# An order of work in the memory stage: the samples' softmax later, their score products in halves

## The chip, the cores and the metric

The kernel runs on one core of a Trainium2 chip. The metric is device microseconds of that core for one launch. Engines: TensorE (PE), VectorE (DVE), ScalarE (ACT), GpSimd (POOL) and SyncE (SP, which here only starts transfers). Each takes its own instructions in order and waits on semaphores for the others.

## The reference

One decoder layer for two groups of requests with shared weights: a prompt of 512 tokens and 8 samples of one token each, width 1024, all in float32. It has a token mixer, cross-attention into 256 memory tokens, and a SwiGLU feed-forward. The change is in the cross-attention:

```
mem_kv:      m = rmsnorm(mem);  mk = m @ w_mk;  mv = m @ w_mv        # 256 tokens, 4 heads of 256; prompt only
mem_attend:  q = h @ w_xq
             s = einsum('bthd,bmhd->bhtm', q, mk) / 16               # scores, per head
             p = softmax(s);  o = einsum('bhtm,bmhd->bthd', p, mv);  return o @ w_xo
```

The prompt's keys and values are computed from `mem_prompt` and are outputs as well. The 8 samples have keys and values of their own in a cache (`cache_mem_k`, `cache_mem_v`), 1 MB per sample and kind.

## The kernel before

**Products.** A float32 product is made of three matmuls on rounded parts, high times high, high times low and low times high. Whatever enters a product is split first: ScalarE writes the high part, VectorE the low one (source minus high). Weights come in slots of 128 x 1024 floats (512 KB): SyncE loads one into one of 2 raw buffers, ScalarE makes its high part in two halves, VectorE its low part, in one of 3 homes. The load of slot s waits until the low part of slot s-2 is made, since they share the raw buffer; the high part of slot s waits until TensorE has used slot s-3. The memory stage has 16 slots in the order of `MEM_TILES`: `mm 0` to `mm 3`, two halves of `mv 0`, `mm 4`, `mm 5`, two halves of `mv 1`, `mm 6`, `mm 7`, and so on. `key_tile(j)` and `split_next(key)` split the slot two places behind the one that they name: `key_tile(2)` on ScalarE and VectorE splits the first half of `mv 0`, `split_next(("mv", 0, 0))` splits `mm 4`.

**The stage.** Eight query tiles (`xq`, 8 slots) come first. Then, on TensorE: `key_tile(j)` makes 128 columns of keys (24 matmuls), two tiles to a head; `mem_scores(h)` the prompt's scores of a head (24 matmuls) into two banks; `key_rows(h)` turns the keys for the output; `value_tile(h)` makes the values from two slots; `turned(h)` transposes the probabilities; `mixed(h)` multiplies them with the values. Around it VectorE takes the maxima (`cmaxes(h)`), ScalarE the exponentials (`cexps(h)`, with the first load of the exponential's table ahead of them), and VectorE scales them (`normalised(h)`). Both have functions of the same names (`key_tile`, `value_tile`, `turned`, `mixed`) for their part of each tile: copy out and high part on ScalarE, low part on VectorE.

**The samples.** Their scores are not made by TensorE. ScalarE writes a head's queries of the 8 samples to memory (`query_rows`), POOL broadcasts them to all partitions (`broadcast_rows`, into 4 buffers `q_by`), and VectorE multiplies with the cached keys and sums (line 2327), two products for a pair of head and sample. `SPREADS` puts the 32 pairs in 9 groups of two parts each; `scores_of(g)` makes group g, three or four pairs, and `spent(engine, g, i)` waits until part i of it is made, when the broadcast buffer and at times a cached key's slot are free. Then the softmax over the samples' scores, which lie over the partitions: `cmx` (a maximum on VectorE), `cmxt` (a transpose on TensorE), the top and `cdiag` (VectorE), `cmxb` (a broadcast by TensorE), `cdif` (a difference on VectorE), an exponential (ScalarE), `csum` (VectorE), `ctot` (a sum over partitions on TensorE), `cpnorm` (VectorE). After it `cached_values(b)` multiplies with the cached values, one sample each.

**What sets the order.** The order is written out by hand, once for each engine (TensorE in lines 3416 to 3500, VectorE 2339 to 2445, ScalarE 1648 to 1690, SyncE 1025 to 1046), and the lists `bank_order`, `val_order` and `split_order` give each result the number that waits count by. There are 7 banks in turn: a result's bank must be free of the one seven places earlier. SyncE's loads of cached keys and values (`load_kv`) stand between those of weights, some behind a wait for products that are made (`spent`), because the values take over slots of keys.

Of the kernel before, what the change touches and what calls it, by code (L numbers as in the profile page):

```python
# [18 lines left out]
ACT = mybir.ActivationFunctionType  # L19
# [4 lines left out]
KD = D // P  # L24
TP = 512
NB = 8
# [143 lines left out]
def bank_order():  # L170

    o = [("gain",), ("xs",)] + [("xt", c) for c in range(5)]
    o += [("in", 0, f) for f in (0, 1)] + [("xt", 6), ("xt", 7), ("bc",)] + [("in", 1, f) for f in (0, 1)]
    o += [("passed", f) for f in (0, 1)]
    for m in range(2, 10):
        o += [("in", m, f) for f in (0, 1)]
        if m == 2:
            o += [("gain2",), ("cp",)] + [("wuk", h) for h in range(NH)]
        if m == 3:
            o += [("rotk", f) for f in (0, 1)]  # L180
        if m == 4:
            o += [("ssq", "nkv")]
        if m == 6:
            o += [("bk",)]
        if m == 8:
            o += [("ct", t) for t in range(4)]
        if m == 9:
            o += [("kt",), ("smp",)]
    o += [("us",), ("ut",)]
    o += [("kn", h) for h in range(NH)]  # L190
    o += [("py", g, f) for g in (3, 2, 1, 0) for f in (0, 1)]
    o += [("ssq", "nq")]
    o += [("ur", p, f) for p in (0, 1) for f in (0, 1)]
    for h in range(NH):
        if h < 2:
            o += [("rotq", h, f) for f in (0, 1)]
        o += [("un", h, f) for f in (0, 1)]
    us = units()
    o += [("s",) + us[0], ("v", 0), ("s",) + us[1], ("qls",), ("v", 1), ("s",) + us[2], ("v", 2), ("qd",), ("s",) + us[3],
          ("v", 3), ("snew",)]  # L200
    for n in range(len(us)):
        o += [("pt",) + us[n]]
        if n + 4 < len(us):
            o += [("s",) + us[n + 4]]
        if n == len(us) - 3:
            o += [("o", 0, 0)]
    o += [("own",)]
    for b in range(NB):
        o += [("sc", b)]
        if b < 3:  # L210
            o += [("o", b + 1, 0)]
    o += [("o", 4, 0), ("o", 5, 0), ("ot",), ("uvs",)]
    for n, m in enumerate(OUT_ORDER):
        o += [("o", m, f) for f in (0, 1) if f or m >= NFIRST]
        if n == MT_AT:
            o += [("mt", k) for k in range(4)]
    def mem_scores(h):
        return [("cs", h, 0), ("cs", h, 1)]

    def mixed(h):  # L220
        return [("cpv", h, 0), ("cpv", h, 1)]

    def turned(h):
        return [("cpt", h, 0), ("cpt", h, 1)]

    for m in range(KD):
        o += [("xq", m, f) for f in (0, 1)]
        if m == 0:
            o += [("ssq", "nxs")]
        if m in (2, 4, 6):  # L230
            o += [("qt", m // 2 - 1)]
        if m == 6:
            o += [("ssq", "nx")]
    o += [("mm", 0), ("qt", 3)] + [("mm", j) for j in (1, 2, 3)]
    o += mem_scores(0) + [("mn", 0)] + [("mv", 0), ("mm", 4), ("cmxt",), ("mm", 5), ("cmxb",)]
    o += mem_scores(1) + [("mn", 1)] + turned(0) + [("mv", 1), ("ctot",)] + mixed(0) + [("mm", 6), ("mm", 7)]
    o += mem_scores(2) + [("mn", 2)] + turned(1) + mem_scores(3) + [("mn", 3), ("mv", 2)] + mixed(1)
    o += turned(2) + [("mv", 3)] + mixed(2) + turned(3) + [("xo", 0, 0), ("cot",)] + mixed(3)
    o += [("xo", m, f) for m in range(KD) for f in (0, 1) if m or f]
    for j in range(J0 - 1):  # L240
        o += [("g", j, 0), ("g", j, 1)]
        if j == 0:
            o += [("ssq", "nf")]
        o += [("u", j, 0)]
        if j == 0:
            o += [("bf",)]
        o += [("u", j, 1)]
    o += [(key, J0 - 1, f) for f in (0, 1) for key in ("g", "u")]
    for j in range(J0, NF):
        o += [("sx", j), ("sy", j), ("sz", j)]  # L250
    for j in range(NF, U_LAST):
        o += [("sx", j), ("sy", j), ("sz", j)] if is_block(j) else [("d", j, m, f) for m in tiles_of(j) for f in (0, 1)]
    o += [("y", 0, 0), ("y", 1, 0), ("e", KD - 2), ("e", KD - 1)] + [("y", t, 0) for t in (2, 3, 4)] + [("y", 0, 1), ("y", 3, 1)]
    o += [("z", 0), ("z", 2), ("z", 4)]
    return o

def val_order():
# [24 lines left out]
    for n, m in enumerate(OUT_ORDER):  # L283
# [2 lines left out]
            o += [("ms", "mem")]  # L286
        if n == MT_AT - 2:
            o += [("memn",)]
    o += [("ms", "nxs"), ("rx",), ("ms", "nx"), ("rxp",), ("cnegm", 0), ("cmx",), ("cdiag",), ("cpn", 0), ("cdif",), ("csum",)]
    o += [("cnegm", 1), ("cpn", 1), ("cpnorm",), ("cnegm", 2), ("cnegm", 3), ("cpn", 2), ("cpn", 3)]  # L290
    for m in range(KD):
        if m == 3:
            o += [("T13", J0)]
# [106 lines left out]
def build(nc, a, consts, outs):  # L400
# [4 lines left out]
    with ctx:  # L405
# [568 lines left out]
        def _(sp):  # L974
# [55 lines left out]
            for i in range(2, len(MEM_TILES) + 2):  # L1030
# [4 lines left out]
                if i == 8:  # L1035
                    spent(sp, 7, 1)
                    load_kv(NB)
                elif i in (9, 10, 11):
                    spent(sp, 8, 1)
                    load_kv(NB + i - 8)  # L1040
                elif i in (12, 13):
                    full(sp, ("cs", 1, 1))
                    load_kv(NB + i - 8)
                elif i in (14, 15):
                    sp.wait_ge(v_used, i - 13)
                    load_kv(NB + i - 8)
# [198 lines left out]
        def _(act):  # L1245
# [16 lines left out]
            def after(key):  # L1262
                act.wait_ge(val, VAL[key] + 1)
# [383 lines left out]

            key_tile(0)
            query_rows(3)
            for j in (1, 2, 3):  # L1650
                key_tile(j)
            split_next(("mv", 0, 0))
            split_next(("mv", 0, 1))
            cexps(0)
            key_rows(0)
            value_tile(0)
            key_tile(4)
            key_tile(5)
            after(("cdif",))
            act.activation(Pcs[:, :, :, :], Dc[:, :, :, :], ACT.Exp, scale=MEM_SCALE).then_inc(c_exp, 1)  # L1660
            cexps(1)
            key_rows(1)
            turned(0)
            value_tile(1)
            mixed(0)
            key_tile(6)
            key_tile(7)
# [257 lines left out]
        def _(dve):  # L1925
# [390 lines left out]
                            gain(G_MEM + 2 * k + 1))  # L2316

            def scores_of(g):

                for i, members in enumerate(SPREADS[g]):
                    slot_ = (2 * g + i) % QBUF
                    dve.wait_ge(q_in[slot_], 16 * ((2 * g + i) // QBUF + 1))
                    for n, (h, b) in enumerate(members):
# [13 lines left out]
            for m in range(KD):  # L2338
# [13 lines left out]
                if m == 6:  # L2352
# [3 lines left out]
                    step(dve.reciprocal(rx[:, 0:4], rx[:, 0:4]))  # L2356
                    dve.tensor_scalar(x_scale[:, 0], rx[:, 0:4], MEM_SCALE, None, ALU.mult).then_inc(rx_made, 1)
                    value(("rxp",), dve.tensor_scalar(x_scale[:, 1], rx[:, 0:4], -MEM_SCALE, None, ALU.mult))
                if m >= 3:
                    scores_of(m - 3)  # L2360

# [34 lines left out]
                for dc in (0, 1):  # L2397
                    low(("cpv", h, dc), A_lo[:, 2 * h + dc, 0:TP], full(dve, ("cpv", h, dc)), A_hi[:, 2 * h + dc, 0:TP])

            for j in range(4):  # L2400
                key_tile(j)
                if j == 3:
                    split_next(("mv", 0, 0))
                scores_of(5 + j)
            cmaxes(0)
            value(("cmx",), dve.tensor_reduce(cols[:, 3], Sc[:, :, :, :].rearrange("p b j h -> p b h j"), AX, ALU.max))
            split_next(("mv", 0, 1))
            b = full(dve, ("cmxt",))
            top = cols[0:NB * NH, 2].rearrange("p b h -> p (b h)")[:, 0:1]
            frees(dve.reduce_max(top, b[0:NB * NH, 0:P], AX), ("cmxt",))  # L2410
            freed(dve, ("cmxt",))
            value(("cdiag",), dve.tensor_scalar(diag[0:NB * NH, :], ident[0:NB * NH, 0:NB * NH], top, None, ALU.mult))
            value_tile(0)
            normalised(0)
            key_tile(4)
            key_tile(5)
            b = full(dve, ("cmxb",))
            frees(dve.tensor_copy(cols[:, 3].rearrange("p b h -> p (b h)"), b[:, 0:NB * NH]), ("cmxb",))
            freed(dve, ("cmxb",))
            value(("cdif",), dve.tensor_tensor(Dc[:, :, :, :], Sc[:, :, :, :], inner(cols[:, 3], 2), ALU.subtract))  # L2420
            dve.wait_ge(c_exp, 1)
            value(("csum",), dve.tensor_reduce(cols[:, 6], Pcs[:, :, :, :].rearrange("p b j h -> p b h j"), AX, ALU.add))
            cmaxes(1)
            turned(0)
            value_tile(1)
            normalised(1)
            mixed(0)
            ins = dve.reciprocal(cols[:, 7].rearrange("p b h -> p (b h)"), full(dve, ("ctot",))[:, 0:NB * NH])
            frees(ins, ("ctot",))
# [428 lines left out]
        def _(pe):  # L2858
# [557 lines left out]
            split(("mt", 3))  # L3416
            key_tile(0)
            query_rows(3)
            for j in (1, 2, 3):
                key_tile(j)  # L3420
            mem_scores(0)
            key_rows(0)
            value_tile(0)
            key_tile(4)
            b = out(("cmxt",))
            after(("cmx",))
            filled(pe.transpose(b[0:NB * NH, 0:P], cols[:, 3].rearrange("p b h -> p (b h)"), ident[:, :]), ("cmxt",))
            key_tile(5)
            b = out(("cmxb",))
            after(("cdiag",))  # L3430
            filled(pe.matmul(b[:, 0:NB * NH], ones[0:NB * NH, :], diag[0:NB * NH, :], start=True, stop=True), ("cmxb",))
            mem_scores(1)
            key_rows(1)
            turned(0)
            value_tile(1)
            b = out(("ctot",))
            after(("csum",))
            filled(pe.matmul(b[:, 0:NB * NH], ones[:, :], cols[:, 6].rearrange("p b h -> p (b h)"), start=True, stop=True), ("ctot",))
            mixed(0)
            key_tile(6)  # L3440
            key_tile(7)
            cached_values(0)
# [297 lines left out]
```

## Time and profile before

| | us |
|---|---|
| median of 3 runs (lowest, highest) | 796.64 (796.23, 796.9) |
| profiled execution | 799.21 |
| its span | 797.4 |
| TensorE busy | 761.1 (95%) |
| VectorE busy | 593.8 (74%) |
| ScalarE busy | 394.2 (49%) |
| POOL busy | 125.9 (16%) |
| mean DMA rate | 138 GB/s |

The profile is of one execution; its times are microseconds from the start of the span. The memory stage lies between 294 and 390 us. A row of a timeline has the start, the time taken, the engine, the line, what is written and read, and in brackets the idle time ahead of it and what ended that.
### The profile page before, as it was taken

To read this page: it belongs to the slowest core of one execution; us is meant where nothing else is said; L and a number is where in the kernel's file an instruction comes from. 1 tells how busy PE (TensorE), PEld (TensorE's weight loads), DVE (VectorE), ACT (ScalarE), POOL (GpSimd) and SP (SyncE) were. 2 spreads that over 40 slices of the span, in tenths; PEclk is the share of its full clock that TensorE was granted. 3 is DMA by queue.
4 is the path that set the end of the run, shared out by engine and by line. 5 is a ranking of instruction groups with operands and counts; after the bars stand their busy time and mean duration, and the time that the engine had idled before them with its cause. 6 is when DMAs were issued, how large, how long until landed. Compare 5 with 4: busy or idle time off the path is not lost. (4 is left out here: it accounts for less than half of the span.)

```text
span 797.4 us, 16199 instructions
## 1 busy us (share of the span) xinstructions
PE 761.1 (95%) x6264; PEld 728.3 (91%) x6264; DVE 593.8 (74%) x1170; ACT 394.2 (49%) x850; POOL 125.9 (16%) x179
## 2 busy tenths in 40 slices
PE   5999998898999998899999999999999999999996
PEld 5999897875899997898899999999999999999996
DVE  5778674677466798666489799888888869876664
ACT  5523776422264433665344356555555558433344
POOL 0376303331004821000046000000000000000000
PEclk9999999999999999899999999999999999999998
DMA  9423333453596668894243214433333333333303
GB/s 266 117 54 86 103 107 143 149 182 136 156 317 221 201 188 242 275 366 164 79 122 107 73 43 116 115 101 108 104 102 106 103 93 107 110 106 117 114 10 108
DMA packets 141521, 109.95 MB, mean 138 GB/s; under 512 B 9477, under 2 KB 133470, under 8 KB 138365
## 3 DMA queue, kind: packets, MB, share of 16 engines
q1 hardware_dynamic: 134574, 90.65, 37.4%
q0 software_dynamic: 3104, 14.68, 5.5%
q10 hardware_dynamic: 3767, 3.59, 1.3%
q8 instruction: 50, 0.82, 0.4%
q14 instruction: 26, 0.21, 0.1%
HBM read 103.93 MB, written 5.20 MB: 137 GB/s over the span
## 5 line engine op out<-in xcount | busy, mean ns | idle before, releaser
L1951 DVE TENSOR_TENSOR wlo<-wraw,whi 128x512 fp32r<-128x512 f32 (+1 forms) x178 | 129.4, 763 | 45.6 <-ACT whi L1254 35.8
L2889 PE MATMUL ps<-B_hi,whi 128*128 128x260 f32 x384 | 110.0, 286 | 3.3 <-DVE xT L1996 1.6
L2891 PE MATMUL ps<-B_hi,wlo 128*128 128x260 f32 x384 | 108.5, 282 | 0.0
L2890 PE MATMUL ps<-B_lo,whi 128*128 128x260 f32 x384 | 108.4, 282 | 0.0
L1254 ACT ACTIVATE whi<-wraw 128x512 fp32r<-128x512 f32 (+1 forms) x138 | 77.8, 615 | 54.6 <-DMA wraw<-in_w_xq_dram 11.4
L2889 PE MATMUL ps<-A_hi,whi 128*128 128x260 f32 x264 | 76.4, 290 | 0.5 <-ACT kn_lo L1348 0.3
L2889 PEld LDWEIGHTS ps<-B_hi,whi 128*128 128x128 f32 x384 | 72.3, 188 | 4.4 <-DVE xT L1996 1.8
L2890 PE MATMUL ps<-A_lo,whi 128*128 128x260 f32 x264 | 75.2, 285 | 0.0
L2891 PE MATMUL ps<-A_hi,wlo 128*128 128x260 f32 x264 | 75.1, 284 | 0.0
L2891 PEld LDWEIGHTS ps<-B_hi,wlo 128*128 128x128 f32 x384 | 72.4, 189 | 0.0
L2890 PEld LDWEIGHTS ps<-B_lo,whi 128*128 128x128 f32 x384 | 72.3, 188 | 0.0
L3526 PE MATMUL ps<-B_lo,whi 128*128 128x260 f32 x236 | 66.6, 282 | 0.0
L3526 PE MATMUL ps<-B_hi,whi 128*128 128x260 f32 x236 | 66.6, 282 | 0.0
L3526 PE MATMUL ps<-B_hi,wlo 128*128 128x260 f32 x236 | 66.6, 282 | 0.0
L1695 ACT ACTIVATE whi<-t 128x512 fp32r<-128x512 f32 x66 | 41.0, 628 | 39.3 <-PE ps L3526 20.6
L2889 PEld LDWEIGHTS ps<-A_hi,whi 128*128 128x128 f32 x264 | 50.5, 191 | 3.0 <-issue 1.7
L1951 DVE TENSOR_TENSOR wlo<-t,whi 128x512 fp32r<-128x512 f32 x66 | 45.3, 687 | 9.4 <-ACT whi L1695 9.4
L2890 PEld LDWEIGHTS ps<-A_lo,whi 128*128 128x128 f32 x264 | 50.4, 191 | 0.1
L2891 PEld LDWEIGHTS ps<-A_hi,wlo 128*128 128x128 f32 x264 | 50.4, 191 | 0.0
L2890 PE MATMUL ps<-h_lo,whi 128*128 128x260 f32 (+1 forms) x164 | 46.3, 283 | 0.0
L3526 PE MATMUL ps<-S_hi,whi 128*128 128x260 f32 x160 | 45.3, 283 | 1.1 <-ACT upv L1760 1.1
L3526 PE MATMUL ps<-S_lo,whi 128*128 128x260 f32 x160 | 45.1, 282 | 0.0
(560 smaller groups left out, 2395.5 us busy)
## 6 DMA issues: line engine op xcount, KB each, us to landing
kv_slot<-in_cache_mem_k_dram SPq DMA_DIRECT2D x8, 1024.0 KB, 8.7
kv_slot<-in_cache_mem_v_dram SPq DMA_DIRECT2D x8, 1024.0 KB, 7.6
wraw<-in_w_out_dram SPq DMA_DIRECT2D x14, 512.0 KB, 4.2
wraw<-in_w_up_dram SPq DMA_DIRECT2D x12, 512.0 KB, 4.5
xraw<-in_w_gate_dram SPq DMA_DIRECT2D x20, 256.0 KB, 3.9
xraw<-in_w_up_dram SPq DMA_DIRECT2D x10, 512.0 KB, 4.1
wraw<-in_w_in_dram SPq DMA_DIRECT2D x9, 512.0 KB, 4.1
wraw<-in_w_gate_dram SPq DMA_DIRECT2D x18, 256.0 KB, 4.4
```

The costliest lines, as they stand in the source:

```text
L1254: act.activation(whi[:, home(s), c0:c1], wraw[:, s % RAW, c0:c1], ACT.Copy).then_inc(w_hi, 1)
L1695: act.activation(piece_at(name, j)[0], piece_source(name, j), ACT.Copy).then_inc(piece_hi, 1)
L1951: return dve.tensor_tensor(dst, src, high.bitcast(F32), ALU.subtract)
L2889: pe.matmul(dst, left[0], right[0], start=first, stop=False)
L2890: pe.matmul(dst, left[0], right[1], start=False, stop=False)
L2891: return pe.matmul(dst, left[1], right[0], start=False, stop=last)
L3526: ins = pe.matmul(b[:, 0:TH], x[:, c], y[:, k, :], start=first and k == n == 0, stop=k == 3 and n == 2, skip_group_check=True)
```

## The change

The order of the same instructions is changed on four engines. The lists of orders at the top change with them; they are left out below.

```diff
 # SyncE
                 if i == 8:
                     spent(sp, 7, 1)
                     load_kv(NB)
-                elif i in (9, 10, 11):
+                elif i in (10, 11):
                     spent(sp, 8, 1)
-                    load_kv(NB + i - 8)
+                    load_kv(NB + 2 * i - 19)
+                    if i == 10:
+                        load_kv(NB + 2)
 # ScalarE
             key_tile(0)
             query_rows(3)
-            for j in (1, 2, 3):
-                key_tile(j)
+            key_tile(1)
+            key_tile(2)
+            cexps(0)
+            key_rows(0)
+            key_tile(3)
             split_next(("mv", 0, 0))
             split_next(("mv", 0, 1))
-            cexps(0)
-            key_rows(0)
             value_tile(0)
             key_tile(4)
             key_tile(5)
-            after(("cdif",))
-            act.activation(Pcs[:, :, :, :], Dc[:, :, :, :], ACT.Exp, scale=MEM_SCALE).then_inc(c_exp, 1)
             cexps(1)
             key_rows(1)
             turned(0)
             value_tile(1)
+            after(("cdif",))
+            act.activation(Pcs[:, :, :, :], Dc[:, :, :, :], ACT.Exp, scale=MEM_SCALE).then_inc(c_exp, 1)
             mixed(0)
 # VectorE
-            def scores_of(g):
-                for i, members in enumerate(SPREADS[g]):
+            def scores_of(g, *parts):
+                for i in parts or (0, 1):
+                    members = SPREADS[g][i]
...
-                if m >= 3:
+                if 3 <= m < KD - 1:
                     scores_of(m - 3)
...
-            for j in range(4):
-                key_tile(j)
-                if j == 3:
-                    split_next(("mv", 0, 0))
-                scores_of(5 + j)
+            key_tile(0)
+            scores_of(4)
+            key_tile(1)
+            scores_of(5, 0)
             cmaxes(0)
+            key_tile(2)
+            scores_of(5, 1)
+            key_tile(3)
+            scores_of(6)
+            split_next(("mv", 0, 0))
+            normalised(0)
+            scores_of(7, 0)
+            split_next(("mv", 0, 1))
+            scores_of(7, 1)
+            value_tile(0)
+            key_tile(4)
+            scores_of(8, 0)
+            key_tile(5)
+            scores_of(8, 1)
             value(("cmx",), dve.tensor_reduce(cols[:, 3], Sc[:, :, :, :].rearrange("p b j h -> p b h j"), AX, ALU.max))
-            split_next(("mv", 0, 1))
+            cmaxes(1)
+            turned(0)
             b = full(dve, ("cmxt",))
...
-            value_tile(0)
-            normalised(0)
-            key_tile(4)
-            key_tile(5)
+            value_tile(1)
             b = full(dve, ("cmxb",))
...
+            normalised(1)
             dve.wait_ge(c_exp, 1)
             value(("csum",), ...)
-            cmaxes(1)
-            turned(0)
-            value_tile(1)
-            normalised(1)
             mixed(0)
 # TensorE
             key_tile(0)
             query_rows(3)
-            for j in (1, 2, 3):
-                key_tile(j)
+            key_tile(1)
+            key_tile(2)
             mem_scores(0)
             key_rows(0)
+            key_tile(3)
             value_tile(0)
             key_tile(4)
+            key_tile(5)
+            mem_scores(1)
+            key_rows(1)
+            turned(0)
...
-            key_tile(5)
+            value_tile(1)
...
-            mem_scores(1)
-            key_rows(1)
-            turned(0)
-            value_tile(1)
+            mixed(0)
...
-            mixed(0)
             key_tile(6)
             key_tile(7)
             cached_values(0)
```

## Rows read from the trace of the kernel before

**Rows 1.** Stretches: their length, then each engine's busy time (instructions), PEclk, DMA share, GB/s.
```profile
296.00:324.40 28.40, 22.52 (x186) 21.68 (x185) 24.95 (x92) 10.50 (x22) 3.44 (x6) 1.00 0.79 246
...
324.80:331.60 6.80, 6.05 (x27) 5.76 (x27) 4.03 (x9) 6.24 (x17) 0.00 (x0) 0.50 0.75 221
...
344.50:392.00 47.50, 47.50 (x424) 40.27 (x423) 26.84 (x47) 25.04 (x56) 0.00 (x0) 1.00 0.54 193
```

**Rows 2.** The timeline of TensorE in the memory stage.
```profile
305.48 0.39 PE L2889 MATMUL ps<-mT_hi,whi 128*128 128x256 f32 x1 [2.18 <-DVE wlo L1951]
...
315.82 0.38 PE L3367 MATMUL ps<-whi,mT_hi 128*128 128x256 f32 x1 [1.20 <-DVE wlo L1951]
...
318.96 0.38 PE L2889 MATMUL ps<-mT_hi,whi 128*128 128x256 f32 x1
...
324.44 0.27 PE L3427 MATMUL ps<-ident,cols 128*32 128x128 f32 x1 [2.39 <-DVE cols L2406]
...
325.55 0.58 PE L2889 MATMUL ps<-mT_hi,whi 128*128 128x256 f32 x1 [0.84 <-DVE wlo L1951]
...
335.77 0.36 PE L3367 MATMUL ps<-whi,mT_hi 128*128 128x256 f32 x1
...
341.64 0.48 PE L2889 MATMUL ps<-PTc_hi,mv_hi 128*128 128x512 f32 x1
...
344.50 0.28 PE L2889 MATMUL ps<-mT_hi,whi 128*128 128x256 f32 x1
```

**Rows 3.** The timeline of VectorE.
```profile
298.86 1.29 DVE L1951 TENSOR_TENSOR wlo<-wraw,whi 128x512 fp32r<-128x512 f32 x2
...
314.46 1.29 DVE L1951 TENSOR_TENSOR wlo<-wraw,whi 128x512 fp32r<-128x512 f32 x2
...
319.28 0.42 DVE L2327 CUSTOM_DVE_ANT_0 prod<-kv_slot,q_by 128x256 f32<-128x256 f32 x1
...
319.75 0.43 DVE L2327 CUSTOM_DVE_ANT_0 prod<-kv_slot,q_by 128x256 f32<-128x256 f32 x1
...
334.59 1.41 DVE L2382 TENSOR_REDUCE cstat<-ps 128x2 f32<-128x512 f32 x2
...
340.22 1.29 DVE L1951 TENSOR_TENSOR PTc_lo<-ps,PTc_hi 128x512 fp32r<-128x512 f32 x2 [4.03 <-ACT PTc_hi L1260]
...
344.23 0.69 DVE L1951 TENSOR_TENSOR mv_lo<-ps,mv_hi 128x512 fp32r<-128x512 f32 x1 [0.26 <-ACT mv_hi L1260]
```

**Rows 4.** The timeline of ScalarE.
```profile
308.45 1.15 ACT L1254 ACTIVATE whi<-wraw 128x512 fp32r<-128x512 f32 x2 [5.42 <-DMA wraw<-in_w_mv_dram]
...
319.95 0.63 ACT L1254 ACTIVATE whi<-wraw 128x512 fp32r<-128x512 f32 x1 [1.86 <-DMA wraw<-in_w_mk_dram]
...
321.13 1.28 ACT L1626 ACT_TABLE_LOAD   x1
...
324.20 0.56 ACT L1626 ACTIVATE Pc<-ps,cstat,x_scale 128x256 f32<-128x256 f32 x1 [1.79 <-DVE cstat L2383]
...
327.46 0.60 ACT L1609 ACTIVATE kv_nat<-ps 128x512 f32<-128x512 f32 x1 [0.48 <-ACT kv_nat L1266]
...
330.37 1.13 ACT L1254 ACTIVATE whi<-wraw 128x512 fp32r<-128x512 f32 x2
...
342.01 1.15 ACT L1254 ACTIVATE whi<-wraw 128x512 fp32r<-128x512 f32 x2 [0.37 <-DMA wraw<-in_w_mk_dram]
```

**Rows 5.** The timeline of SyncE, which issues the loads.
```profile
300.18 0.37 SPq L982 DMA_DIRECT2D wraw<-in_w_mv_dram  x1
...
319.34 0.51 SPq L1015 DMA_DIRECT2D kv_slot<-in_cache_mem_v_dram  x1
...
325.52 0.37 SPq L982 DMA_DIRECT2D wraw<-in_w_mv_dram  x1
...
333.45 0.37 SPq L982 DMA_DIRECT2D wraw<-in_w_mk_dram  x1
```

**Rows 6.** DMA issues of the page: form, count, KB each, median us to landing.
```profile
kv_slot<-in_cache_mem_v_dram SPq DMA_DIRECT2D x8, 1024.0 KB, 7.6
```

More of the change, by code:

```diff
@@ L233, in bank_order @@
             o += [("ssq", "nx")]
-    o += [("mm", 0), ("qt", 3)] + [("mm", j) for j in (1, 2, 3)]
-    o += mem_scores(0) + [("mn", 0)] + [("mv", 0), ("mm", 4), ("cmxt",), ("mm", 5), ("cmxb",)]
-    o += mem_scores(1) + [("mn", 1)] + turned(0) + [("mv", 1), ("ctot",)] + mixed(0) + [("mm", 6), ("mm", 7)]
+    o += [("mm", 0), ("qt", 3), ("mm", 1), ("mm", 2)]
+    o += mem_scores(0) + [("mn", 0), ("mm", 3), ("mv", 0), ("mm", 4), ("mm", 5)]
+    o += mem_scores(1) + [("mn", 1)] + turned(0) + [("cmxt",), ("mv", 1), ("cmxb",)] + mixed(0) + [("ctot",), ("mm", 6), ("mm", 7)]
     o += mem_scores(2) + [("mn", 2)] + turned(1) + mem_scores(3) + [("mn", 3), ("mv", 2)] + mixed(1)
@@ L288, in val_order @@
             o += [("memn",)]
-    o += [("ms", "nxs"), ("rx",), ("ms", "nx"), ("rxp",), ("cnegm", 0), ("cmx",), ("cdiag",), ("cpn", 0), ("cdif",), ("csum",)]
-    o += [("cnegm", 1), ("cpn", 1), ("cpnorm",), ("cnegm", 2), ("cnegm", 3), ("cpn", 2), ("cpn", 3)]
+    o += [("ms", "nxs"), ("rx",), ("ms", "nx"), ("rxp",), ("cnegm", 0), ("cpn", 0), ("cmx",), ("cnegm", 1), ("cdiag",), ("cdif",)]
+    o += [("cpn", 1), ("csum",), ("cpnorm",), ("cnegm", 2), ("cnegm", 3), ("cpn", 2), ("cpn", 3)]
     for m in range(KD):
```

## The prediction, written before the result was known

> **What bounds it now.** I read the stretches first, then each engine in order of time, with what ended its waits. From 344.5 to 392 us TensorE is busy for every microsecond. Before that it is not: 22.5 of 28.4 us from 296 to 324.4 us, and from 324.8 to 331.6 us it runs at the lower of its two clock levels, 1.2 GHz (a granted clock of 0.50), 27 matmuls in 6.05 us of busy time against 186 in 22.5 us [rows 1]. Its waits are 2.18 us ahead of `key_tile(3)`, 1.20 us inside `value_tile(0)`, both for low parts of weights from VectorE, 2.39 us at `cmxt` for `cmx`, and 0.84 us ahead of `key_tile(5)` for a low part again [rows 2]; together 6.6 us, and the change is about these. VectorE is late with them: a score product starts every 0.47 us (319.28, 319.75), so a (head, sample) pair costs 0.93 us and a group of four pairs 3.7 us, and such a group stands ahead of the next low part, as ahead of that at 314.46 [rows 3].
>
> But another chain ends last. `cmaxes(1)` starts at 334.59, its exponentials follow on ScalarE, and the low parts of the turned probabilities, started at 340.22, end at 341.51; `mixed(0)` starts at 341.64 [rows 2, 3]. So some of the 6.6 us and of the slow clock is already hidden by this chain. What counts is when TensorE starts `key_tile(6)`, now 344.50 [rows 2], since after it nothing holds TensorE [rows 1]: a delay there goes to the end one for one.
>
> **The change, followed through.** No product or copy is added or taken away; TensorE, VectorE, ScalarE and SyncE get a new order, and POOL's broadcasts go as their buffers come free. I write the new times on the old scale, with old durations and landing times.
>
> 1. Group 4 leaves the last query tile and goes behind the weights' low part that now starts at 298.86. That one can start at 296.1 and end at 297.4. The load of the first `mv` weights waits for it: now issued at 300.18 and landed at 308.45, 8.3 us [rows 3, 4, 5], then issued at 297.5 and landed at 305.8.
>
> 2. TensorE ends `key_tile(2)` at 303.3 as now (305.48 less the wait, [rows 2]) and goes to `mem_scores(0)`, whose second key's low part is ready at 303.5. It ends at 306.5, `cmaxes(0)` at 307.5, `key_tile(3)` at 309.8. The wait of 2.18 us shrinks to about 0.5.
>
> 3. ScalarE's `cexps(0)` now stands ahead of `key_tile(3)`. So the next weights' high part (its load goes out at 303.2 and is in by 311.7 even at 8.5 us) stands behind the table load, 1.28 us, and exponentials with `key_rows(0)`, 3.3 us from 324.20 to 327.46 [rows 4]. From 307.6 that is 312.2; the high and low parts end at 314.1. TensorE waits 1.6 us inside `value_tile(0)` and starts its second half at 314.1 instead of 315.82.
>
>    The trace has the table load at 321.13 with 1.28 us, then a wait for `cnegm` to 324.20 [rows 4]; this leaves room for anything up to 3.1 us. The Trainium skill, page "ScalarE: Activation LUTs", section "What ACT_TABLE_LOAD costs", says that a switch of set also pays a drain of about 1.38 us. The old order would have hidden it, the new one would not. An estimate with that page's figure is 1.4 us more on the whole sum; no row here shows the drain.
>
> 4. `key_tile(4)`: from 314.1 VectorE makes the key's low part (0.35), three pairs (2.8) and the weights' low part (1.25), to 318.5; now the tile starts at 318.96. `key_tile(5)`: normalising (1.35), two pairs (1.87) and a low part (1.25) more, 322.9 against 325.55. With scores and transposes TensorE is through `turned(0)` at 330.0, now at 335.77 [rows 2]. So far 5.7 us are won.
>
> 5. Then `cmxt` waits for `cmx`, which has all products of group 8 ahead of it. SyncE's queue holds these up: behind the first `mv(1)` load stands a wait for group 7 (`spent(sp, 7, 1)`), long satisfied when it was reached at 319.34 [rows 5]. Now group 7 ends at 324.7, the 1 MB cache load goes at 324.8, and only behind it, at 325.5, the second `mv(1)` load. Now that load is issued at 325.52 and lands by 330.37, when ScalarE comes to it without a wait [rows 4, 5]. With these 4.9 us it lands at 330.4; high part, low part and the key's low part end at 332.7, two pairs at 334.5, `cmx` at 334.7. TensorE waits 4.7 us and starts `value_tile(1)` at 334.9: 0.9 us won, no longer 5.7.
>
> 6. `cmaxes(1)` starts at 334.7, as now (334.59). Its exponentials, `key_rows(1)` and the turned parts are unchanged: 341.5. But now the top and `cdiag` stand behind them (0.5 us) and `cmxb` waits for it, so `mixed(0)` starts at 342.1 instead of 341.64 and ends at 345.0.
>
> 7. `csum` was done at 334.6, ahead of `cmaxes(1)`. Now it stands behind `value_tile(1)`, the copy of `cmxb` with `cdif` (0.45), `normalised(1)` (1.35) and itself (0.2): 2.0 us behind the low part of `mv(1)`, which now ends at 344.92 [rows 3]. This alone puts `csum` at 346.9, 2.4 us behind the 344.50 of `key_tile(6)`. It gets later: the weights that VectorE and ScalarE must split before that low part land at 342.01, issued at 333.45, 8.5 us [rows 4, 5]. Their load now stands behind two 1 MB cache loads held for group 8 (334.5): issued at 335.7, landed at 344.2, low part of `mv(1)` done at 347.2, `csum` at 349.1. TensorE waits 4.2 us for it at `ctot`, and `key_tile(6)` starts at 349.3.
>
> Sum on the old durations: 349.3 - 344.5 = +4.8 us.
>
> **Two costs that the rows don't fix.** *The landing behind a cache load* (step 5). At the least it is the 4.9 us of its own row, where nothing was ahead of it; at the most about the 8.5 us of the load at 333.45, with cache loads around it [rows 5]. A cache load by itself takes 7.6 us in the median [rows 6]. I take the middle, 6.7, so +1.8 us, passed on whole, as `cmx`, `cmaxes(1)` and SyncE's wait for group 8 all move; the ends are 0 and +3.6. The Trainium skill, page "DMA: Bandwidth & Descriptors", section "Queues, rings and completion order", says that the descriptors of one ring are taken in order; by that the load would not be in ahead of the cache load's 332.4, 6.9 us from its issue, and the sum 0.2 us more.
>
> *The clock.* The waits of 2.39 and 0.84 us stood ahead of the fall to 1.2 GHz, where a matmul took 0.22 us instead of 0.12, so a tile of 24 some 2.5 us more [rows 1, 2]. The wait at `cmxt` is longer and should do the same, that at `ctot` may. Of the first, most hides under the late landing of step 7; I count 0.8 of the 2.5 us. The second would lie in the open on `key_tile(6)`, 1.7 to 2.6 us; I leave it to the range. With no fall it is 0. A gain is excluded: the old fall was hidden by the chain of `mixed(0)`.
>
> Forecast: 4.8 + 1.8 + 0.8 = +7.4 us. The profiled execution took 799.21 us (span 797.4), so 806.6; it stands 2.6 us above the median of the runs, 796.64, and the same step from there gives 804.0 us.
>
> **Rivals.**
> - *The loads land sooner (faster).* The load behind the low part at 314.46 is in at 319.95, 4.2 us after that part's end [rows 3, 4]. If all weights' loads do that, as they may when they are asked for earlier, steps 3, 5 and 7 shorten: `cmx` at 333, the low part of `mv(1)` at 342.3. It decides from the point where `csum` is done before 344.5, 4.6 us sooner than in my sum; then TensorE keeps what step 4 won. I get -0.6 us from the weights, -1.6 with quick caches: 795.0 us. For it: landings range from 4.2 to 8.5 us. Against: the same bytes move. 11%.
> - *The gains and the late `csum` cancel.* The load of step 5 takes 4.9 us and that of step 7 some 5: 4.8 - 3.5, about +1, 797.6 us. For it: with nothing ahead the rows do show 4.9. 9%.
> - *Only the late `csum`.* No fall of the clock, landings as in the trace: +1.6 to +4.8, some 800 us. 17%.
> - *Everything adds.* Both falls and 8.5 us for the load: 4.8 + 3.6 + 0.8 + 2.1 = +11.3, 807.9 us. For it: the longest wait now did bring a fall. 13%.
> - The forecast, +4.8 to +9.5 (801.4 to 806.1 us): 50%. That the products don't move is no rival, since the order is written out.
>
> **How the numbers follow.** A measurement of this kernel tells 0.2% (1.6 us) from nothing. Faster 0.11, same 0.09, slower 0.17 + 0.13 + 0.50 = 0.80. The range is 796.5, with half of the cancelling case in, to 808.5; left out are the faster case, half of the same and a tail above. The likeliest case's own range is 801.4 to 806.1.
>
> **What would show it.** A wait of about 0.5 us ahead of `mem_scores(0)` (step 2); some 1.6 us inside `value_tile(0)`, with VectorE waiting for a high part that ScalarE made behind its exponentials (3); TensorE's longest wait at `cmxt`, 4 to 7 us, with the second `mv(1)` load issued right behind a cache load (5); 3 to 5 us at `ctot` for `csum` (7); 1.2 GHz in `value_tile(1)`. If `ctot` waits under 1 us, step 7 is wrong and with it the sign. If the wait at `cmxt` is short, what holds group 8 was misread.

## The result, and the profile of the changed kernel

| | before | changed |
|---|---|---|
| median of the runs on one chip (lowest, highest) | 796.77 us (796.23, 799.54) | 808.88 us (807.37, 812.17) |
| profiled execution, span | 799.21, 797.4 us | 807.37, 805.6 us |
| last matmul of the query tiles to the last of `mixed(3)` | 95.7 us | 105.8 us |

The ratio is 1.0137, with a 95% interval of 1.0116 to 1.0159: the change costs 10.9 us (9.2 to 12.7). All ratios here are those of the record, and they can differ from the quotient of two medians: these two lie 12.1 us apart. In this execution the stage begins 1.89 us earlier than in the one before (the last matmul of the query tiles starts at 292.39, not 294.29), so 1.89 us are added wherever times are compared with the rows of before; this is called the old scale. The stage alone is 10.0 us longer; less the 1.89 us, that is the whole difference between the two spans, 8.2 us.

TensorE's timeline of the changed kernel, to be laid beside [rows 2]:

```profile
301.98 0.39 PE L2901 MATMUL ps<-mk_hi,q_hi 128*128 128x256 f32 x1 [0.61 <-DVE mk_lo L1954]
...
312.04 0.38 PE L3379 MATMUL ps<-whi,mT_hi 128*128 128x256 f32 x1 [0.92 <-DVE wlo L1954]
...
316.38 0.38 PE L2901 MATMUL ps<-mT_hi,whi 128*128 128x256 f32 x1 [1.25 <-DVE wlo L1954]
...
320.79 0.39 PE L2901 MATMUL ps<-mT_hi,whi 128*128 128x256 f32 x1 [1.43 <-DVE wlo L1954]
...
334.34 0.37 PE L3444 MATMUL ps<-ident,cols 128*32 128x128 f32 x1 [6.27 <-DVE cols L2423]
...
342.23 0.50 PE L2901 MATMUL ps<-PTc_hi,mv_hi 128*128 128x512 f32 x1
...
349.87 0.39 PE L3452 MATMUL ps<-cols,ones 128*128 128x32 f32 x1 [4.61 <-DVE cols L2438]
...
350.29 0.56 PE L2901 MATMUL ps<-mT_hi,whi 128*128 128x256 f32 x1
...
358.38 1.07 PE L3424 MATMUL ps<-kv_slot,Pv_pad 128*32 128x256 f32 x16
```

The four small waits are those of steps 2 to 4. The two long ones are what the change made: 6.27 us at `cmxt`, where 2.39 us were, and 4.61 us at `ctot`, where there was none (L3444 and L3452). `key_tile(6)` starts 57.9 us after the last query tile, 50.2 before: 7.7 us later. And `key_tile(6)` with `key_tile(7)` takes 8.09 us (350.29 to 358.38), where it took 5.74 (344.50 to 350.24). 7.7 + 2.35 is the 10.0.

The stretches say why the second part is there. The columns are those of [rows 1]: behind the busy times come the granted clock, the DMA share and GB/s.

```profile
331.50:338.30 6.80, 3.96 (x19) 3.97 (x20) 4.01 (x14) 2.76 (x10) 0.00 (x0) 0.50 0.49 165
338.40:348.40 10.00, 6.86 (x46) 5.83 (x44) 5.33 (x13) 4.50 (x10) 0.00 (x0) 1.00 1.04 388
348.50:355.30 6.80, 5.43 (x25) 5.46 (x26) 4.11 (x8) 2.04 (x5) 0.00 (x0) 0.50 1.00 379
358.38:400.00 41.62, 41.62 (x375) 34.52 (x375) 20.63 (x36) 21.18 (x48) 0.00 (x0) 1.00 0.39 128
```

Before, one stretch of 6.8 us ran at 1.2 GHz, behind the waits of 2.39 and 0.84 us [rows 1, 2]. Now there are two, each around one of the long waits, and the second covers nearly all of `key_tile(6)`. Then TensorE is busy to the end of the stage, as before.

VectorE, ScalarE and SyncE around these waits, to be laid beside [rows 3], [rows 4] and [rows 5]:

```profile
330.57 1.29 DVE L1954 TENSOR_TENSOR wlo<-wraw,whi 128x512 fp32r<-128x512 f32 x2 [3.36 <-ACT whi L1256]
...
333.98 0.22 DVE L2423 TENSOR_REDUCE cols<-Sc 128x32 f32<-128x64 f32 x1
334.11 1.41 DVE L2386 TENSOR_REDUCE cstat<-ps 128x2 f32<-128x512 f32 x2
...
345.64 0.69 DVE L1954 TENSOR_TENSOR wlo<-wraw,whi 128x512 fp32r<-128x512 f32 x1 [2.96 <-ACT whi L1256]
...
348.37 1.22 DVE L2394 TENSOR_TENSOR Pc<-Pc,cstat 128x1024 f32<-128x1024 f32 x1
349.51 0.21 DVE L2438 TENSOR_REDUCE cols<-Pcs 128x32 f32<-128x64 f32 x1
```

```profile
303.44 1.15 ACT L1256 ACTIVATE whi<-wraw 128x512 fp32r<-128x512 f32 x2 [2.01 <-DMA wraw<-in_w_mv_dram]
305.33 1.28 ACT L1628 ACT_TABLE_LOAD   x1
306.63 0.57 ACT L1628 ACTIVATE Pc<-ps,cstat,x_scale 128x256 f32<-128x256 f32 x1
...
329.84 0.63 ACT L1256 ACTIVATE whi<-wraw 128x512 fp32r<-128x512 f32 x1 [4.91 <-DMA wraw<-in_w_mv_dram]
...
344.98 1.15 ACT L1256 ACTIVATE whi<-wraw 128x512 fp32r<-128x512 f32 x2 [3.81 <-DMA wraw<-in_w_mk_dram]
```

```profile
295.67 0.37 SPq L982 DMA_DIRECT2D wraw<-in_w_mv_dram  x1
...
322.50 0.34 SPq L1015 DMA_DIRECT2D kv_slot<-in_cache_mem_v_dram  x1
322.89 0.43 SPq L982 DMA_DIRECT2D wraw<-in_w_mv_dram  x1
...
334.83 0.43 SPq L982 DMA_DIRECT2D wraw<-in_w_mk_dram  x1
335.31 2.60 SPq L1015 DMA_DIRECT2D kv_slot<-in_cache_mem_v_dram  x1
```

Read backwards: `ctot` waits for `csum` (349.51), which stands behind `normalised(1)` (348.37) and the low part at 345.64, which waited 2.96 us for a high part, which waited 3.81 us for weights issued at 334.83: 10.15 us, behind two cache loads. The same holds one wait earlier: `cmxt` waits for `cmx` (333.98), that for the products behind the low part at 330.57, that for weights issued at 322.89 right behind a cache load and taken at 329.84, 6.95 us. "Taken" is when ScalarE starts on a load; the trace has the landing itself too, here at 344.95 and 329.82.

### The profile page after: what moved, and what is told of

It is laid out like the page before. It is cut to its first block and busy times, and to the rows that moved or that the text cites. A ratio compares the mean times of both kernels' runs of the same rounds, so it can differ in the third digit from the quotient of the medians.

```text
span 805.6 us, 16200 instructions
## 1 busy us (share of the span) xinstructions
PE 760.2 (94%) x6264; PEld 726.9 (90%) x6264; DVE 593.3 (74%) x1170; ACT 394.2 (49%) x850; POOL 126.2 (16%) x179
```

## The experiments

The kernel before ran on the same chip with each group: its median was 798.7 us for the first four runs by number, 798.3 for the next four, 798.1 for the ninth and tenth, 798.6 for the last two. The runs are told in the order of the argument. A gain or loss in us is the ratio less one, times 798.

**One part of the change alone, in the kernel before.** The eleventh run moves `csum` and `ctot` only:

```diff
 # VectorE                       # TensorE
-csum                            -ctot
 cmaxes(1)                        mixed(0)
 turned(0)                       +ctot
 value_tile(1)                    key_tile(6)
 normalised(1)
+csum
```

> The kernel before with one part of the change alone: csum stands behind value_tile(1) and normalised(1) on VectorE, and ctot behind mixed(0) on TensorE; everything else is as before. Theory (step 7 of the prediction, its part without late loads): VectorE ends normalised(1) at 346.3 on the scale of the profile before, csum at 346.5, TensorE waits 1.9 us at ctot, and the kernel is 1.9 to 2.3 us slower, ratio 1.0025; if the wait also brings a fall of the clock, 4 us, ratio 1.005. Rival (ctot is hidden by something that was late anyway, so that only the loads and the clock made the change slow): no difference, ratio 1.000.

The twelfth adds the changed kernel's order of cache loads:

```diff
-elif i in (9, 10, 11):
+elif i in (10, 11):
     spent(sp, 8, 1)
-    load_kv(NB + i - 8)
+    load_kv(NB + 2 * i - 19)
+    if i == 10:
+        load_kv(NB + 2)
```

> As the run before it, and with the changed kernel's order of SyncE's loads (value 1 behind the load of mm 6, with value 2 right behind it, so that the load of mm 7 stands behind two cache loads). Theory (the load of mm 7 sets VectorE's low part ahead of csum): that load takes 10 us instead of 8.5, the low part, normalised(1) and csum come 1 to 3 us later, TensorE waits 3 to 5 us at ctot, the clock falls on key_tile(6), and the kernel is 1.5 to 5 us slower than the run before it, ratio to the kernel before 1.004 to 1.009. Rival (the order of the loads costs nothing by itself; the 10 us in the changed kernel came from the late start of group 8): as the run before it within 1 us.

Measured: 801.58 us, ratio 1.0035 (1.0007 to 1.0063), and 805.85 us, 1.0094 (1.0071 to 1.0116). TensorE in the eleventh, then in the twelfth:

```profile
346.29 0.38 PE L3439 MATMUL ps<-cols,ones 128*128 128x32 f32 x2 [2.19 <-DVE cols L2426]
...
346.50 0.36 PE L2889 MATMUL ps<-mT_hi,whi 128*128 128x256 f32 x1
...
352.34 1.07 PE L3412 MATMUL ps<-kv_slot,Pv_pad 128*32 128x256 f32 x16
```

```profile
345.84 0.61 PE L3441 MATMUL ps<-cols,ones 128*128 128x32 f32 x2 [4.70 <-DVE cols L2428]
...
346.26 0.56 PE L2891 MATMUL ps<-mT_hi,whi 128*128 128x256 f32 x1
...
354.33 1.07 PE L3414 MATMUL ps<-kv_slot,Pv_pad 128*32 128x256 f32 x16
```

In the eleventh `key_tile(6)` starts at 346.50 instead of 344.50. This execution's stage begins 0.93 us later than that of the kernel before, but by `cmxt` both are level (324.46, 324.44), and so is VectorE's low part behind it (332.16, 332.14). So the late `csum` by itself costs 2.0 us, and the clock holds (the pair of key tiles takes 5.84). In the twelfth the load of `mm 7` goes out at 330.52 and is taken at 341.31, 10.8 us later, where the eleventh's took 8.3 (333.47 to 341.75). The wait grows to 4.70 and the pair takes 8.07 us. Its stage begins 3.08 us earlier than before, so its `key_tile(6)`, 55.05 us after the last query tile, is 4.8 us later than the 50.2 of before; with the 2.3 us of the pair that is 7.2. The stretch from 344.60 on in the eleventh and the twelfth:

```profile
344.60:351.40 6.80, 5.11 (x43) 5.14 (x44) 4.82 (x11) 2.62 (x6) 0.00 (x0) 1.00 1.03 382
```

```profile
344.60:351.40 6.80, 5.56 (x26) 5.59 (x27) 3.98 (x8) 1.15 (x2) 0.00 (x0) 0.51 1.03 395
```

So two edits, neither of which touches the score products, make 7.5 of the 10.9 us. The rivals are out: that `ctot` would be hidden (the interval of the eleventh run lies above 1, if only just), and that the order of the loads costs nothing (4.7 us between the two runs).

**The wait at ctot, in the changed kernel.** The fourth run puts `ctot` behind `key_tile(6)`:

```diff
 mixed(0)
-ctot
 key_tile(6)
+ctot
 key_tile(7)
```

> One edit to the changed kernel: TensorE does key_tile(6) ahead of ctot. Theory (the wait at ctot lies in the open on TensorE, and nothing behind it needs ctot before cached_values(0)): key_tile(6) fills 2.9 us of the wait of 4.6 us and the clock may stay up, 2.4 us more: +5.5 to +8 on before. Rival (the wait would only reappear at cached_values(0) or in the next scores, behind VectorE's cpnorm and its split of the weights): same as the changed kernel within 1 us.

805.95 us, 1.0101 (1.0056 to 1.0146): 8.1 us instead of 10.9, with intervals that overlap. The profile shows the mechanism: no wait at `ctot`, `key_tile(6)` 54.1 us after the last query tile (57.9), the pair of tiles in 5.96 us. Only a stretch of 10.2 us at 1.2 GHz around the wait at `cmxt`, 7.87 us here, is left. Not all of this is the edit's: the load of `mm 7` took 8.3 us in this execution and `csum` was made at 348.74, so that in its old place `ctot` would have waited some 2.6 us (from the end of `mixed(0)` at 346.5), not 4.6.

**The loads, in the changed kernel.** The first run puts the cache load behind the second `mv(1)` load, the second run all later ones behind that of `mm 7`, the third does both:

```diff
-if i == 8:            # first and third
+if i == 9:
     spent(sp, 7, 1)
     load_kv(NB)
-elif i in (10, 11):   # second and third
+elif i == 11:
     spent(sp, 8, 1)
-    ...
+    for b in (1, 2, 3):
+        load_kv(NB + b)
```

> One edit to the changed kernel: SyncE waits for group 7 and loads the first cached values behind the second load of mv(1), not ahead of it. Theory (TensorE's 6.3 us at cmxt come from that load, issued late and right behind 1 MB): the load is issued about 1.5 us sooner and lands in about 5 us instead of 7, cmx is ready 3.6 us sooner, the wait at cmxt falls to some 3 us, and the time goes from about 10.9 us above the kernel before to some 7. Rival (the score products themselves, VectorE's work, hold cmx): the wait at cmxt stays at 5 us or more and the time where the changed kernel's is, +10 to +12.

> One edit to the changed kernel: SyncE waits for group 8 and loads cached values 1 to 3 (3 MB) behind the load of mm 7, not two of them ahead of it. Theory (the 4.6 us at ctot are for the most part this load, 10 us from issue to landing): it is issued as soon as the second low part of mv(1) is made and lands before VectorE asks for it, csum comes some 3.7 us sooner, the wait at ctot is 1 to 2 us, and TensorE's clock doesn't fall there; the time is some 6 us less than the changed kernel's, +5 on before. Rival (csum is late by its place on VectorE, behind value_tile(1) and normalised(1)): the wait at ctot stays at 3.5 us or more, +9 to +11.

> Both edits of SyncE's order in the changed kernel. Theory: they act on different waits, so they add: cmxt some 3 us, ctot some 2 us, one fall of the clock at most in the stage; +1 to +3 on before. Rival (VectorE's order alone): still +8 or more.

804.87 us, 1.008 (1.0048 to 1.0112); 805.33, 1.0074 (1.0049 to 1.01); 801.94, 1.0027 (1.0002 to 1.0052). The first halves the wait at `cmxt` (2.93 us) and leaves that at `ctot` (4.89); the second leaves `cmxt` (6.36) and cuts `ctot` to 1.33, and the key tiles take 5.8 us again. Together they take back 8.8 of the 10.9 us. The third's profile has 3.05 at `cmxt`, 1.40 at `ctot`, and a wait that the changed kernel's profile has not:

```profile
317.36 0.58 PE L3378 MATMUL ps<-whi,mT_hi 128*128 128x256 f32 x1 [3.50 <-DVE wlo L1953]
...
336.36 0.27 PE L3443 MATMUL ps<-ident,cols 128*32 128x128 f32 x1 [3.05 <-DVE cols L2422]
...
348.49 0.38 PE L3451 MATMUL ps<-cols,ones 128*128 128x32 f32 x2 [1.40 <-DVE cols L2437]
```

None of these edits comes ahead of it. The load of the first `mv` weights took 11.0 us there (issued 297.77, taken 308.77), 7.8 in the changed kernel's profile; all that ScalarE does behind it, exponentials included, shifted. The changed kernel's profile is the exception in this: of the eight profiles that have its order up to that load (its own and the first six and the tenth run's), two show 7.7 and 7.8 us and six 10.9 to 11.9, with 1.7 to 2.4 us of wait ahead of `mem_scores(0)`. One profile is one draw of these landings, so the runs' medians, not the profiles, carry the verdicts here. The third run's clock was not as expected either: 6.8 us at 1.2 GHz in `value_tile(0)` and 3.4 us behind `cmxt`, two falls and not one.

**The start of the stage.** The fifth run puts ScalarE's `key_tile(3)` ahead of `cexps(0)` again; the seventh loads the last cached key one weights' load later (`if i == 4` for `if i == 3`).

```diff
+key_tile(3)
 cexps(0)
 key_rows(0)
-key_tile(3)
```

> One edit to the changed kernel, half of its ScalarE part undone: ScalarE does key_tile(3), with the high part of the second half of mv(0), ahead of cexps(0). Theory (step 3: that high part stands behind the table load and the exponentials, and more so when the load two slots ahead lands late): the wait inside value_tile(0) goes (1 us in the changed kernel's trace, 3.5 us where that load took 11 us), and the time falls by 1 to 3 us against the changed kernel. Rival (the wait comes back ahead of key_tile(4) or at cmxt, as VectorE has the same work): within 0.7 us of the changed kernel, whose runs lie near 1.0137 of before.

> One edit to the changed kernel: the 1 MB load of the last cached keys goes behind the load of the first mv weights, not ahead of it. Theory (the time from that load's issue to its landing, 7.8 us in the changed kernel's trace and 11 us in another, is its place behind 1 MB): it lands in about 5 us, ScalarE reaches its exponentials as soon as VectorE has made the maxima, the wait in value_tile(0) is 1 us or less in every execution, and the time falls by 1 to 3 us against the changed kernel with less spread. Rival (group 6 then waits for its keys, or the landing is set by other transfers): no change or slower.

808.66 us, 1.0127 (1.0108 to 1.0145), and 808.43, 1.0111 (1.0086 to 1.0136): no gain that can be told, where 1 to 3 us were expected of each. In both the wait only moved, to the next low part (1.88 us ahead of `key_tile(4)`; 1.62 in `value_tile(0)`, where the seventh's second `mv(0)` load took 9.0 us), and `cmxt` still waited 6.2 and 6.4 us.

**The samples' softmax in VectorE's gap.** The sixth run brings `cmxb`, `cdif`, the exponential and `csum` forward, behind `cmaxes(1)`, where VectorE waits 4 us for ScalarE, and `ctot` ahead of `mixed(0)`:

```diff
 # VectorE: behind cmaxes(1)
+cmxt's top, cdiag; copy of cmxb; cdif; csum
 turned(0)
 value_tile(1)
 normalised(1)
 # TensorE: cmxb between the halves of value_tile(1)
-mixed(0)
 ctot
+mixed(0)
```

> The changed kernel with the samples' softmax put into the 4 us in which VectorE waits for ScalarE's exponentials of head 1: top, cdiag, the copy of cmxb, cdif and csum come right behind cmaxes(1) on VectorE; cmxb stands between the halves of value_tile(1) and ctot ahead of mixed(0) on TensorE; its exponential behind cexps(1) on ScalarE. SyncE's order as in the changed kernel. Theory (the wait at ctot is csum's place on VectorE as well as the late load of mm 7): no wait for csum; mixed(0) waits about 1 us for its own operands, and the late load of mm 7 costs only what reaches key_tile(6) or 7. Some 4 us less than the changed kernel, 6 if the clock stays up: +5 to +7 on before. Rival (mm 7's load alone): a wait of the same 4 us appears ahead of mixed(0) or key_tile(7), and nothing is won.

804.64 us, 1.0082 (1.0061 to 1.0102), 4.4 us better than the changed kernel. The wait at `ctot` and the second fall of the clock are gone (the pair of key tiles: 5.7 us); 6.2 us at `cmxt` stay. In its place `mixed(0)` waits 0.73 us.

**All together, and a version that beats both.** The eighth run has the edits of the third, fifth, sixth and seventh, and group 8 whole ahead of `key_tile(5)` on VectorE, which no run tries alone. The ninth spreads the cached values besides; the tenth is the ninth without the fifth's and the seventh's edits.

```diff
 elif i == 11:
     spent(sp, 8, 1)
-    for b in (1, 2, 3):
-        load_kv(NB + b)
-elif i in (12, 13):
+    load_kv(NB + 1)
+elif i == 12:
+    load_kv(NB + 2)
+elif i == 13:
+    load_kv(NB + 3)
     full(sp, ("cs", 1, 1))
-    load_kv(NB + i - 8)
+    for b in (4, 5):
+        load_kv(NB + b)
```

> All of it together: both loads of weights ahead of the cached values, the cached keys' load behind the first mv load, key_tile(3) ahead of cexps(0) on ScalarE, group 8 of the products whole and ahead of key_tile(5) on VectorE, and the samples' softmax in VectorE's gap. Theory: what is left in TensorE's stage are waits under 2 us ahead of key_tile(4), key_tile(5), cmxt and mixed(0), some 7 us in all with no long one, and no fall of the clock but perhaps one; 2 to 4 us faster than the kernel before, ratio 0.995 to 0.998. Rival (the change's order cannot beat the old one, since VectorE has the same work in both): at or above 1.000.

> As the eighth run (all four moves together), and now one cached value's load goes behind each of the weights' loads that follow (values 1, 2, 3 behind the loads of mm 7, the first and the second half of mv 2; values 4 and 5 behind that second half as well), where values 1 to 3 went together behind mm 7 and value 4 ahead of the second half of mv 2. Theory (the late landings behind cache loads are what is left): the second half of mv 2 lands in 5 to 6 us instead of 8.5, ScalarE's wait of 7.2 us for it shrinks to about 4, TensorE's wait of 2.0 us ahead of mem_scores(3) to under 0.5, and the time comes to some 796.8 us where the kernel before has 798.4: ratio 0.998. Rival (the same megabytes only come later and hold up the next load or a cached value): a wait of 1 to 3 us comes back at value_tile(2) or at a cached value, ratio 1.000.

> As the run before it, without two of the four moves: the last cached key's load stands ahead of the load of the first mv weights again, and ScalarE makes its exponentials ahead of key_tile(3) again, as in the changed kernel. Theory (the start of the stage hangs on ScalarE getting the first mv weights late, and with nothing late behind it this is no longer hidden): TensorE waits 3 to 5 us in value_tile(0) and at key_tile(4) together, cmxt waits 2 to 3, and the time is 1 to 3 us above the run before it, ratio 1.000 to 1.002. Rival (the waits at the start are hidden behind group 8 as they were in the changed kernel): the same time as the run before it within 1 us.

The eighth: 798.64 us, 1.0004 (0.9988 to 1.002), not the 2 to 4 us faster that were expected. Its `key_tile(6)` starts 48.6 us after the last query tile, 1.6 sooner than before the change. But ScalarE then waits 7.17 us for weights that stand behind three cached values (the first half of `mv 2`, not the second as the ninth run's expectation has it; issued at 338.38, 9.6 us), TensorE 2.01 us ahead of `mem_scores(3)`, and the lead is gone. The ninth, where that load takes 4.0 us: 796.54 us, 0.9971 (0.9953 to 0.999), 2.3 us faster than the kernel before; this is the best one. TensorE in it:

```profile
311.54 0.39 PE L3380 MATMUL ps<-whi,mT_hi 128*128 128x256 f32 x1 [0.59 <-DVE wlo L1956]
...
318.05 0.39 PE L2902 MATMUL ps<-mT_hi,whi 128*128 128x256 f32 x1 [3.49 <-DVE wlo L1956]
...
331.16 0.27 PE L3449 MATMUL ps<-ident,cols 128*32 128x128 f32 x1 [1.51 <-DVE cols L2423]
...
338.87 0.50 PE L2902 MATMUL ps<-PTc_hi,mv_hi 128*128 128x512 f32 x1 [0.66 <-DVE PTc_lo L1956]
...
341.72 0.28 PE L2902 MATMUL ps<-mT_hi,whi 128*128 128x256 f32 x1
```

Nothing over 0.7 us is left behind `cmxt`, and the wait ahead of `mem_scores(3)` is gone. The tenth: 799.59 us, 0.9999 (0.9977 to 1.0021). So the late start of the stage, worth nothing in the changed kernel (fifth and seventh runs), seems to be worth about 2 us once nothing behind it is late; the two intervals overlap. No run gives the kernel before the ninth's order of loads, so how much of the 2.3 us comes from the change's own order, and how much from the loads alone, isn't shown.

## Why the prediction came out as it did

The sign and the mechanism were right, the size was too small: +7.4 us against 10.9. The median of 808.88 us lies just beyond the upper end of 808.5; the ratio on the 796.64 us that the range stands on gives 807.6, just inside. By its steps, in times on the old scale:

| step | predicted | measured |
|---|---|---|
| 1: first `mv` load issued, taken | 297.5, 305.8 | 297.56, 305.33 |
| 2: wait at `mem_scores(0)` | 0.5 | 0.61 |
| 3: second half of `value_tile(0)`, and the wait ahead of it | 314.1, 1.6 us | 313.93, 0.92 us |
| 4: `key_tile(4)`, `key_tile(5)` | 318.5, 322.9 | 318.27, 322.68 |
| 4: end of `turned(0)` | 330.0 | 329.96 |
| 5: second `mv(1)` load, issue to taken | 6.7 us | 6.95 us |
| 5: `value_tile(1)` behind `cmxt` (with the 1.8) | 336.7 | 336.36 |
| 6: `mixed(0)` (with the 1.8) | 343.9 | 344.12 |
| 7: load of `mm 7`, issue to taken | 8.5 us | 10.15 us |
| 7: wait at `ctot` | 4.2 us | 4.61 us |
| start of `key_tile(6)` | +7.4 us | +7.7 us |
| `key_tile(6)` and `key_tile(7)` | unchanged | +2.35 us |

**Steps 1 to 4** hold within 0.5 us in their times, and in part by luck: in six of the eight profiles the first `mv` load takes some 3 us longer, with a wait of 1.7 to 2.4 us, not 0.5, in step 2. Step 3 was the place for a rule: the drain that the Trainium skill, page "ScalarE: Activation LUTs", section "What ACT_TABLE_LOAD costs", adds to a switch of set. The row shows the table load at 305.33 with 1.28 us, right behind a copy that began at 304.90 and took 0.42, and the first exponential at 306.63, 0.02 us behind its end. An estimate with the page's 1.38 us has it start at 308.0. The measurement decides: the open 1.28 us were the whole price, as the sum had it.

**Step 5** holds, but its price was met by luck. The load behind the cache load took 6.95 us, and the cache load stood 0.39 us ahead of it. The lower bound of my two was misread: 4.9 us is when ScalarE came to the load of before, which had landed after 3.4. And the 7.6 us for a cache load by itself did not hold here:

```profile
L1015 SPq DMA_DIRECT2D kv_slot<-in_cache_mem_v_dram x1: 341/341/341, 322.5 to 322.5; - x1
DMA to landing us min/median/max: 5.4/5.4/5.4
```

It landed at 327.90, and the weights at 329.82, 1.9 us behind it. The Trainium skill, page "DMA: Bandwidth & Descriptors", section "Queues, rings and completion order", says that the descriptors of one ring are taken in order. The order of these two landings agrees with it; the 6.9 us that I worked out by it do not rest on it, since with the 5.4 us it gives only 5.0 as the least. The first run shows the other side: with that order turned round the load lands in 3.3 us, and the wait at `cmxt` falls from 6.27 to 2.93 us.

**Step 7** holds in kind, and its first half, the late `csum` by itself, was worked out as 2.4 us and measured alone as 2.0 (eleventh run). Its second half was too small: two cache loads ahead made the load of `mm 7` take 10.15 us (10.8 in the twelfth run, though 8.3 in the fourth), not the 8.5 carried over from a row with one fewer right ahead of it. The landings come one behind the other: 338.95 and 342.91 for the two cache loads, 344.95 for the weights.

**The clock** is the term that was mis-sized: the sum had 0.8 us for the first fall, in `value_tile(1)`, and nothing for the second, which cost 2.35. The first did happen (`value_tile(1)` took 7.42 us, 334.47 to 341.89, where it took 5.74 before), and delayed `mixed(0)`, but nothing of it reached `key_tile(6)`, since VectorE set that time through `csum`; the term came out right by luck, because the load of `mm 7` was later by about as much. The second fall I had put at 1.7 to 2.6 us and left to the range. The rows of before had a wait of 2.39 with one of 0.84 behind it, and a fall [rows 1, 2]; a lone wait of 4.2 us, on the path, should have carried that fall in the forecast itself. The last two runs bear it out: a wait of 2.19 us there leaves the tiles at 5.84 us, one of 4.70 makes 8.07. With it the forecast is +9.8, 806.4 us; the "everything adds" case was the nearest.

What stays open: 0.9 us between the profile's 10.0 and the ratio's 10.9 lies inside the interval; the profiled execution was also the fastest of the four. And why the landings of one and the same load differ by 3 us between profiles of kernels with the same order up to there (7.8 and 11.0 us) isn't settled; it makes the start of the stage vary, and the fifth and seventh runs found no single load that carries it.

## What to carry to other kernels

A wait that a change shortens is worth only what the next wait behind it leaves: here 5.8 us were won ahead of `cmxt`, and all of them were lost again behind a load that stood behind a guarded transfer. In a queue in order, ask of every wait that guards a transfer what is behind it, and put what is needed first ahead of it; the order that cost 10.9 us became part of one that gains 2.3 once the loads and the small chain through `csum` followed it. Price a wait of several microseconds on TensorE as the wait and the slow tile behind it. And where landings vary by 3 us, take a load's time from several profiles, and from the landing and not from when it is taken.

## What the runs showed of the hardware

A 512 KB load with nothing unfinished ahead of it in SyncE's queue landed in 3.4 us (issued at 325.52 in the kernel before). The second `mv(1)` load, right behind one 1 MB load, took 6.9 to 7.1 us in five profiles and 8.4 in the fourth run's; the load of `mm 7`, right behind two, took 9.7 to 10.8 us in six profiles and 8.3 in the fourth run's. The first `mv` load of the changed order took 7.7 to 7.8 us in two profiles and 10.9 to 11.9 in six.

A wait of 4.6 to 4.7 us at `ctot` went with 6.8 us at 1.2 GHz, which cost 2.3 us of a tile pair that takes 5.7 us; one of 2.2 us at the same place cost no clock at all. But the length of the wait alone does not decide it. In the same profile, the eleventh run's, an equal wait ahead of `key_tile(3)` was followed by 3.4 us at 1.2 GHz:

```profile
306.72 0.38 PE L2889 MATMUL ps<-mT_hi,whi 128*128 128x256 f32 x1 [2.19 <-DVE wlo L1951]
```

```profile
308.20:311.60 3.40, 3.40 (x18) 3.40 (x17) 3.26 (x12) 1.84 (x4) 1.07 (x2) 0.50 0.81 285
```

In the kernel before, 2.18 us there cost nothing: from 305.4 to 315.8 its granted clock was 1.00. Two places with waits of 2.0 us, ahead of `mem_scores(0)` in the first run and of `mem_scores(3)` in the eighth, brought 3.4 us at 1.2 GHz each.

A table load for the exponential on ScalarE cost its 1.28 us and nothing more: in the ninth run too the load starts at 311.35 and the exponential at 312.64.
